# The forgetting-attention kernel: another order of the query blocks in the second half of each pair's steps

## The reference, cut to what matters

```python
def fox_attend(q, k, v, cq, ck, qpos, kpos):
    s = jnp.einsum('bqhd,bkhd->bhqk', q, k).astype(jnp.float32) * FOX_SCALE
    decay = jnp.swapaxes(cq, 1, 2)[:, :, :, None] - jnp.swapaxes(ck, 1, 2)[:, :, None, :]
    causal = kpos[None, :] <= qpos[:, None]
    p = jax.nn.softmax(jnp.where(causal, s + decay, NEG), axis=-1)
    return jnp.einsum('bhqk,bkhd->bqhd', p.astype(v.dtype), v)
...
    for l in range(DEPTH):
        h = rms_norm(xp, ln_mix[l])
        qa, ka, va, la, qb, kb, vb = project_heads(h, w_in[l], b_f[l])
        ...
        o = jnp.concatenate([fox_prompt(qa, ka, va, la), swa_prompt(qb, kb, vb, swa_sinks[l])], axis=-1)
        xp = xp + o @ w_out[l]
```

## Time and profile before

| | |
|---|---|
| median of 3 runs | 3757.86 us |
| lowest and highest | 3747.61 and 3765.87 us |
| profiled execution, device time | 3755.0 us |
| its span from first to last instruction | 3753.2 us |
| its mean granted TensorE clock | 0.958 of full speed |
| PE busy | 3437.0 us (92%) |
| PE weight loads busy | 3290.0 us (88%) |
| DVE busy | 1913.1 us (51%) |
| ACT busy | 862.3 us (23%) |
| GpSimd busy | 1190.7 us (32%) |

### The profile page before, as it was taken

One profiled execution on the slowest core, in us unless ns is written; L12 is line 12 of the kernel. 1 busy time (PEld: TensorE's weight loads), 2 busy tenths in 40 slices (PEclk: granted clock), 3 DMA queues, 4 the chain that ended last, 5 costly groups with the idle time before them and its releaser, 6 DMA issues. The chain is left out here.

```text
span 3753.2 us, 52839 instructions
## 1 busy us (share of the span) xinstructions
PE 3437.0 (92%) x21112; PEld 3290.0 (88%) x21112; DVE 1913.1 (51%) x3568; ACT 862.3 (23%) x1994; POOL 1190.7 (32%) x976
## 2 busy tenths in 40 slices
PE   6998998779889999999989999988788999999997
PEld 6888887668889999999978888877788899999997
DVE  5443445566664443444554444455676644444445
ACT  4331332343330000000132322223443200000001
POOL 4023112125244333333441122112442433333431
PEclk9899999879999999999989999988799999999998
DMA  4112111012111111111121111101110111111111
GB/s 143 37 29 63 46 36 52 21 43 71 29 37 43 46 43 46 43 44 42 46 65 46 47 40 55 45 27 32 60 51 27 42 46 43 43 45 43 46 45 62
DMA packets 85254, 175.53 MB, mean 47 GB/s; under 512 B 10400, under 2 KB 13600, under 8 KB 84608
## 3 DMA queue, kind: packets, MB, share of 16 engines
q1 hardware_dynamic: 72112, 133.03, 11.9%
q10 hardware_dynamic: 12896, 38.97, 3.5%
HBM read 150.23 MB, written 16.29 MB: 44 GB/s over the span
## 5 line engine op out<-in xcount | busy, mean ns | idle before, releaser
L583 POOL TENSOR_TENSOR WH<-RAW,zero 128x512 fp32r<-128x512 f32 x484 | 546.3, 1129 | 2477.1 <-PE PS L603 2464.6
L603 PE MATMUL PS<-HH,WH 128*128 128x384 f32 (+1 forms) x3216 | 851.8, 335 | 104.0 <-DVE T L1500 31.2
L603 PE MATMUL PS<-HL,WH 128*128 128x384 f32 (+1 forms) x3216 | 836.9, 330 | 0.0
L603 PE MATMUL PS<-HH,WL 128*128 128x384 f32 (+1 forms) x3216 | 835.7, 330 | 0.0
L603 PEld LDWEIGHTS PS<-HH,WH 128*128 128x128 f32 x3216 | 576.3, 190 | 126.6 <-DVE T L1500 37.1
L585 POOL TENSOR_TENSOR WL<-RAW,WH 128x512 fp32r<-128x512 f32 x484 | 649.0, 1341 | 37.9
L603 PEld LDWEIGHTS PS<-HL,WH 128*128 128x128 f32 x3216 | 579.7, 190 | 0.0
L603 PEld LDWEIGHTS PS<-HH,WL 128*128 128x128 f32 x3216 | 578.4, 190 | 0.0
L1654 DVE TENSOR_TENSOR XT<-PS,XT 128x320 f32<-128x320 f32 (+1 forms) x512 | 346.6, 718 | 315.4 <-PE PS L603 315.3
L603 PE MATMUL PS<-G0H,WH 128*128 128x384 f32 (+1 forms) x1056 | 298.4, 338 | 34.6 <-DVE XT L1654 14.9
L1087 ACT ACTIVATE PTH<-PS 128x512 fp32r<-128x512 f32 (+4 forms) x320 | 165.4, 520 | 627.9 <-PE PS L603 625.8
(11 more groups left out here) (212 smaller groups left out, 5223.2 us busy)
## 6 DMA issues: line engine op xcount, KB each, us to landing
RAW<-in_slabs SPq DMA_DIRECT2D x484, 256.0 KB, 2.6
XR<-decays ACTq DMA_DIRECT2D x16, 512.0 KB, 5.8
XT<-in_xT SPq DMA_DIRECT2D x8, 544.0 KB, 8.0
XR<-decays ACTq DMA_DIRECT2D x16, 272.0 KB, 6.8
out_fk<-T ACTq DMA_DIRECT2D x8, 544.0 KB, 2.7
out_fv<-T ACTq DMA_DIRECT2D x8, 544.0 KB, 3.3
RX<-T ACTq DMA_DIRECT2D x32, 136.0 KB, 3.5
out_y<-YT ACTq DMA_DIRECT2D x8, 544.0 KB, 3.1
```

The costliest lines, as they stand in the source:

```text
L583: pool.tensor_tensor(WH[:, s, :], RAW[:, s, :], zero[:, 0:1].to_broadcast([128, HALF]), ALU.add).then_inc(w_hi, 1)
L603: ins = pe.matmul(*a, **k)
```

## The change

The list of blocks for the second half becomes 7, 4, 6, 5, 2 with 3, 0 with 1. The heads stay as they were for each block (in the second half, 7, 6 and 5 belong to head 1, the others to head 0). The first half is as before. So steps 8 to 12 were [0, 1], [6], [2, 3], [5], [4] and are now [4], [6], [5], [2, 3], [0, 1].

```diff
             steps = []
             order = []
-            blocks = [[7], [0, 1], [6], [2, 3], [5], [4]]
-            for h in range(2):
-                order += [(1 - h if k % 2 else h, b) for k, b in enumerate(blocks)]
+            for h, blocks in enumerate(([[7], [0, 1], [6], [2, 3], [5], [4]], [[7], [4], [6], [5], [2, 3], [0, 1]])):
+                order += [(1 - h if b in ([0, 1], [2, 3], [4]) else h, b) for b in blocks]
             for h, b in order:
```

## The result

The changed kernel takes 3769.69 us in the median of 16 runs (3761.36 to 3792.89), the kernel before 3753.38 us in the median of 16 (3747.61 to 3766.61). The ratio is 1.005, 95% interval 1.0037 to 1.0062: slower by 14 to 23 us. Forecast were 15.0 us more, and measured are 16.3. (The 3773 us of the prediction stood on a median of three runs, 3757.9; the sixteen runs have the kernel before at 3753.4, and 15.0 more than that is 3768.4.)

The account below looks back on a forecast made before the run. PE, busy 92% of the span, was taken to bound the kernel, so only its waits could change. 5.9 + 0.3 + 3.5 + 1.5 + 1.7 + 2.1 = 15.0 us on 3757.9 gave 3773 us, range 3758 to 3788.

Parts of the forecast that it names:

- The tail: From q2's end: fewer value matmuls beside the chain, 6 x 0.99 = 5.9 us more; wider G0L behind pair 1, 0.3 us.
- Behind pair 3: Chain from the swap DMAs, where no queries follow: 0 us, bounds -0.3 and +0.99 us for each of the two.
- Group B of step 8: Step 8's new second transpose group waits for copies of step 7's: 0.44 us, eight times, 3.5 us.
- Group B of step 10: Step 10's second transpose group waits for copies of step 9's: 0.19 us, eight times, 1.5 us.
- The wait for q1: PE's wait ahead of q1 grows by 0.21 us with wider copies of step 11's second group: eight times, 1.7 us.
- The wait for q2: Six transposes in step 12, not ten, ahead of q2 open a wait of 0.26 us: eight times, 2.1 us.
- The clock: PE's granted clock behind the six long waits: by the sum these waits cost their length alone.
- rival 1: Half-clock stretch behind the six long waits gets longer, 3 to 10 us more: 3776 to 3783 us; chance 22%.
- Rival 2: Chain from q2's end gets 1 us shorter, so the 5.9 us go and 9 remain: 3767 us; chance 12%.
- Rival 3: Not slower: the 0.75 us wait ahead of q1 closes, 6.0 us gained, 3752 us with a shorter chain; chance 5%.
- Rival 4: The change doesn't do what it says: 3758 us; chance 3% together with the rest.

Follow-up runs that it names:

- e2_last7: Kernel before with blocks 7 and 4 of the second half swapped (4, 01, 6, 23, 5, 7): 3744.90 us, ratio 0.9978.
- e4_q1: Kernel before with steps 10 and 11 of the second half swapped (7, 01, 6, 5, 23, 4): 3756.42 us, ratio 1.0007.
- e3_swap_last: Changed kernel with its last two steps swapped (7, 4, 6, 5, 01, 23): 3764.59 us, ratio 1.0034 to the kernel before.
- e6_swap_4_01: Changed kernel with steps 10 and 11 in the old order (7, 4, 6, 23, 5, 01): 3773.43 us, ratio 1.0053 to the kernel before.
- e5_best: Second half reordered to 5, 6, 23, 4, 01, 7, against the kernel before: 3747.07 us, ratio 0.9977.
- e8_after_again: The changed kernel run again unedited, against the kernel before: 3770.11 us, ratio 1.0064.

## Why the prediction was right, point by point

**The bound.** Right: PE's waits are what the order moved. The other engines' better or worse spread in the middle shows in no wait but those named below.

**The tail.** Right. Forecast 0.99 us in six tails and 0.14 more behind pair 1; measured 1.04 (QSL 3.00 to 4.04) and 1.18 (G0L 3.31 to 4.49). e2_last7 shows the same mechanism with the other sign.

**Behind pair 3.** Forecast nothing. The wait for G0L grew from 0.68 to 0.92 us there, and the wait inside `down` that followed shrank, 1.41 in the earlier trace rows against 0.97. From the issue of the swap DMAs to PE's start behind that wait it is 10.15 us (599.75 to 609.90) and was 10.37, inside the bounds that were given:

```profile
600.62 0.62 PE L602 MATMUL PS<-G0H,WH 128*128 128x384 f32 x2 [0.92 <-DVE G0L L1476]
609.90 0.41 PE L602 MATMUL PS<-G0H,WH 128*128 128x320 f32 x1 [0.97 <-DVE XT L1653]
```

**Group B of step 8.** Right: 0.44 us forecast and measured. The look of it was off: 0.3 to 0.5 shown was announced, 0.23 is shown, since more of the wait lies under the modelled end of the transpose before it.

**Group B of step 10.** Forecast 0.19. It isn't shown as a wait at all, only as a longer row: 12 transposes last 1.53 us to k0, and 1.31 in e4_q1, where nothing holds them. 0.22 us.

**The wait for q1.** Forecast +0.21, measured 0.97 - 0.75 = +0.22.

**The wait for q2.** Forecast +0.26. The six transposes last 322.98 - 322.10 = 0.88 us to q2, where ten take 1.03 and six alone would take 0.62: 0.26 us.

```profile
322.10 0.83 PE L602 MATMUL PS<-ident,PR 128*128 128x128 f32 x6
322.98 0.41 PE L602 MATMUL PS<-HH,WH 128*128 128x320 f32 x1
```

**The sum.** Eight times 0.44 + 0.22 + 0.22 + 0.26 = 1.14 are 9.1 us, the tails 4 x 1.04 + 2 x 1.18 = 6.5: 15.6 us, forecast 15.0, and the medians differ by 16.3. A pair in which the clock stayed up confirms it: from step 7's reduction to PE's start behind the wait for QSL, pair 2 of the second layer takes 66.00 us and took 63.70. That is 2.30 us more, and the terms give 1.14 + 1.04 = 2.18; the slower second matmul behind a wait is a part of the rest. So the terms were right one by one. That the total came within 1.3 us of the forecast is in part luck: e3_swap_last and e6_swap_4_01 came out 6 to 7 us above what their waits give. The ratio's 14 to 23 us leave some microseconds beyond.

**The clock.** The prediction took nothing for the clock, and rival 1 up to 10 us behind the six long waits. Rival 1 didn't happen there: the half-clock stretches at these six waits add up to 24 and 20 us in the changed kernel's two profiles, and to 27 us in both of the kernel before, so they didn't grow with the waits. Half-clock stretches stand at places that the prediction didn't name, in the middle of the second half, where PE hardly waits, and at q1. They make the times spread upwards (3788.53 and 3792.89 at a mean clock of 0.953 and 0.952) more than they move the median. A share of the clock in the average loss isn't shown: the means differ by 17.6 us in the first batch and by 20.7 in the second, 2 and 5 us more than the waits, but the mean granted clock over all executions is 0.958 in the changed kernel (24) and 0.957 in the kernel before (43).

**The other rivals.** Rival 2 (a shorter chain) didn't happen: QL took 2.09 us for 2.03. Rival 3 (the wait for q1 closes) didn't, for the reason given there; in the runs it closed where step 11 has no second group, as in e3_swap_last and e5_best. Rival 4 is out.

## What to carry to other kernels

In a software pipeline that is bound by one engine, the order of unequal pieces doesn't change that engine's work, only what it has at hand while fixed chains on other engines run: find the chain at the end (here the splitting of the next queries, 5 us) and put the largest piece beside it, not the smallest. Ahead of a piece that must wait for the copies of a large neighbour, put one with enough work behind its first group; ahead of a copy that someone waits for, put a piece that has no second group. Both together gave orders that beat both kernels, such as 23, 6, 5, 4, 01, 7, at a ratio of 0.9970 (0.9956 to 0.9984) to the kernel before. The largest block at the end alone gave 0.9978 (0.9964 to 0.9993), so by the times the end is what counts, and the rest is seen in the waits.

## What was not expected of the hardware

The granted TensorE clock fell to half in the middle of back-to-back matmuls, with PE busy 13.00 of 13.00 us and no wait of more than 0.23 us in the ten microseconds ahead (narrow ones: value products of 128 columns, transposes, and scores of a few hundred columns). One such stretch cost 6.1 us, about what all six tails lost together. So two executions of one kernel needn't take the same time (3761.74 and 3801.99 us in e8_after_again, at clocks of 0.960 and 0.947), and a profile of one execution can show a total that its waits don't explain. Before such a stretch is put down to a change, look for it in the parts that the change left alone.
